# Both feed-forwards with other operands on TensorE, two norm boundaries that walk tokens 128-255 ahead, and a context scaled apart

## The chip, the cores and the metric

The kernel runs on one core of a Trainium2 chip. The metric is the device time of one execution in microseconds; lower is better. A core has a matrix engine (TensorE, PE in the profile), a vector engine (DVE), a scalar engine (ACT), GpSimd (POOL) and SyncE (SP, which here only issues transfers), an on-chip memory of 128 partitions and 8 accumulation banks of 128 x 512 f32 (PSUM, the tensor `ps`). Each engine works through its own instructions in order; semaphores are all that ties them together.

## What is computed

Two transformer blocks on 256 tokens of width 2048, in f32. The first has causal attention with 8 heads beside a gated 31-tap convolution, and a SwiGLU feed-forward; the second has neighbourhood attention with 16 heads on the tokens and 256 context tokens, and a feed-forward with a 3-tap convolution along the tokens:

```python
h = rms_norm(x, mix_pre_g) * (1 + sc1) + sh1
x = x + g1 * rms_norm(hybrid_mixer(h, ...), mix_post_g)
h = rms_norm(x, ffn_pre_g) * (1 + sc2) + sh2
x = x + g2 * rms_norm((silu(h @ w_gate) * (h @ w_up)) @ w_down, ffn_post_g)
# second block
h, hc = modulate(rms_norm(x), sh1, sc1), modulate(rms_norm(ctx), csh1, csc1)
x = x + g1 * neighbourhood_attention(h, hc, ...)
hf = modulate(rms_norm(x), sh2, sc2)
gate, up = split(dwconv3(hf @ w_up, conv_w, conv_b))
x = x + g2 * ((silu(gate) * up) @ w_down)
```

The shifts, scales and gates (sh, sc, g) are products of a vector with `ada_w`, 2048 x 12288 for each block. The hidden widths are 5632 and 5504.

## The kernel before

**Tiles of weights.** All weights pass through as tiles of 128 x 1024 f32 (512 KB). SP loads a tile into one of four `raw` slots once the low part of the tile four before is made (L352 to L365). ACT rounds it into `w_hi` (`hi`, L678, the operation is L683) once TensorE is done with the tile four before; DVE makes `w_lo = raw - w_hi` (`lo`, L1172, the operation is L1175). TensorE waits for `lo_ready`, uses the tile and raises `tile_used`. Activations are split in the same way, and a product is three matmuls: hi*hi, hi*lo, lo*hi.

**Three forms of product.** `columns_tile` (L1890, matmuls L1903 to L1905) holds a 128x128 block of weights in the array and moves the 256 tokens of `h` past it; the result has channels on the partitions. `chunk_tile` (L1858, matmuls L1873 to L1875) holds 128 tokens and moves 512 columns of weights; the result has tokens on the partitions. `row_product` (L2148, L2157 to L2159) is the same for the products `w_out` and `w_down`, one tile per 128 rows of the weight and half of the output columns. Before, both feed-forwards' gate and up products use `columns_tile`: 22 chunks of 512 columns each, 8 tiles a chunk. A loop trip of 16 tiles (`gate_up_1`, L2218) does one up and the next gate chunk.

**What is woven in.** Beside the tiles run the products of `ada_w` ("units", L1177 to L1188): SP loads 512 KB into one of two `ada` slots, DVE multiplies by the condition and adds into `acc0`, `acc1` or, for the context, `tmp` too (two operations). The schedule of units per tile is written out by hand in SP's and DVE's programs, 12 units a trip in the first two trips of the first feed-forward, 8 later. TensorE sums an accumulator over the partitions at the end (`sum_rows` L1933, `sum_columns` L1923). POOL builds the table of the second attention's bias: 16 small loads into `tab`, 8 writes of a broadcast to memory (L630), 8 skewed reads (L637), two masks (L642, L645) and a write (L647). It starts when the first boundary's x is ready.

**A boundary.** Between a `w_out` or `w_down` product and the next stage the kernel needs statistics of y (two norms), the update of x, statistics of x, and h. `last_rows` (L2162) finishes the last four tiles for tokens 128-255 first (`later_done`), then for tokens 0-127. ACT (`boundary`, L900) takes sums of squares (L882, L889, L896) and roots, DVE (L1504) updates x (L1495 to L1502) and makes a diagonal matrix of 1/rms for each half (`make_diag`, L1234); both do tokens 128-255 and then 0-127, and only then splits and h. TensorE turns x by products with the diagonals into columns (`scaled_rows`, L1941, matmul L1950), ACT scales and shifts them (`modulated`, L711, L722), DVE splits them (L1247, L1249), and `first_chunk` (L1954) starts. An f32 matmul leaves two records in the profile, a transpose one. For the second block, `first_chunk` also turns the context by diagonals behind its last tiles, and then `sum_rows` makes a gate.

**The second feed-forward's evacuation.** ACT makes the middle tap (L1124) and DVE the two outer ones (L1775, L1781) from PSUM; then `silu`, the product, and at the end `down_phase` stages its first rows (L864, L1432).

## Time and profile before

| | us |
|---|---|
| median of 3 runs | 2795.03 |
| fastest and slowest run | 2790.72, 2800.84 |
| the profiled execution | 2799.87 |
| its span, first to last instruction | 2798.2 |

| engine | busy | share |
|---|---|---|
| TensorE | 2669.5 | 95% |
| DVE | 1827.2 | 65% |
| ACT | 1275.3 | 46% |
| POOL | 143.6 | 5% |

The transfers moved 623 MB, 223 GB/s on average. Busy time of TensorE is a union of overlapping durations: a matmul's duration holds the way through the array, so its pace is read from the starts. The granted clock of TensorE, averaged over the span, was 0.976 of 2.4 GHz. The stages, in us from the start of the span: mixer to 403, its output product to 524, first feed-forward (gate and up) to 1108, down product to 1370, second block's attention to 1916, its output product to 2035, second feed-forward to 2550, down product to the end.

### The profile page before, as it was taken

The page shows a single profiled execution, that of the slowest core. Times are in us where ns is not written, and L with a number is a line of the kernel's source. Part 1 is how long each engine was busy: PE and PEld are TensorE (multiplying, and loading weights), DVE is VectorE, ACT ScalarE, POOL GpSimd, SP SyncE. Part 2 cuts the span into 40 slices and gives each one's busy share as a digit, 9 for nine tenths or more (in the row PEclk, how much of TensorE's full clock was granted, in tenths as well). Part 3 has the DMA queues.
Part 4 walks back from the last instruction along what each step waited for, and adds up shares of the span by engine and source line. Part 5 has one row for each costly group of instructions (what it writes and reads, how often), then busy time and mean ns, then how long its engine had stood idle before and what let it go on. Part 6 is the DMA issues. An engine that isn't in the chain of part 4 may idle for free.

```text
span 2798.2 us, 45510 instructions
## 1 busy us (share of the span) xinstructions
PE 2669.5 (95%) x16790; PEld 2343.3 (84%) x16790; DVE 1827.2 (65%) x2258; ACT 1275.3 (46%) x1850; POOL 143.6 (5%) x226
## 2 busy tenths in 40 slices
PE   7989898988999999999999999999999999999999
PEld 4677777888899999877777878787889999998887
DVE  2339778657788786768765555555568765656565
ACT  2349645532334243454643343434455545555553
POOL 3101011102000000000000010100000000000000
PEclk9999999999999999999999999999999999999999
DMA  9978587599788587678554454554448866655554
GB/s 342 387 271 296 187 285 248 177 291 275 257 274 274 201 282 253 223 257 299 181 172 159 161 163 153 179 176 138 160 167 287 276 193 181 183 170 177 192 192 165
DMA packets 238963, 623.03 MB, mean 223 GB/s; under 512 B 20005, under 2 KB 24256, under 8 KB 238009
## 3 DMA queue, kind: packets, MB, share of 16 engines
q1 hardware_dynamic: 210738, 519.18, 56.0%
q0 software_dynamic: 27040, 95.96, 10.4%
q10 hardware_dynamic: 1072, 6.35, 0.6%
q8 instruction: 74, 1.21, 0.2%
q14 instruction: 39, 0.32, 0.0%
HBM read 613.80 MB, written 7.60 MB: 222 GB/s over the span
## 4 chain that ended last, share of the span: by engine, by line
PE 82%; DMA 7%; DVE 5%; ACT 3%; issue 2%; SPq 0%; ACTq 0%; DVEq 0%; POOL 0%; POOLq 0%
PE ps L1903 12%; PE ps L1904 12%; PE ps L1905 12%; PE ps L2157 7%; PE ps L2158 7%; PE ps L2159 7%; PE ps L1873 6%; PE ps L1875 6%; PE ps L1874 6%; DMA ada<-in_ada_w 2%; PE ps L1986 2%; DMA raw<-in_w_up 1%; PE ps L1929 1%; ACT w_hi L683 1%; PE ps L2091 1%
## 5 line engine op out<-in xcount | busy, mean ns | idle before, releaser
L1175 DVE TENSOR_TENSOR w_lo<-raw,w_hi 128x1024 fp32r<-128x1024 f32 x766 | 938.7, 1229 | 716.9 <-ACT w_hi L683 715.7
L683 ACT ACTIVATE w_hi<-raw 128x1024 fp32r<-128x1024 f32 x766 | 811.0, 1060 | 1167.9 <-PE ps L1905 496.1
L1903 PE MATMUL ps<-h_hi,w_hi 128*128 128x256 f32 x3296 | 950.3, 288 | 36.2 <-DVE w_lo L1175 29.3
L1904 PE MATMUL ps<-h_lo,w_hi 128*128 128x256 f32 x3296 | 940.5, 285 | 0.0
L1905 PE MATMUL ps<-h_hi,w_lo 128*128 128x256 f32 x3296 | 940.0, 285 | 0.0
L1903 PEld LDWEIGHTS ps<-h_hi,w_hi 128*128 128x128 f32 x3296 | 640.5, 194 | 76.7 <-DVE w_lo L1175 36.8
L1904 PEld LDWEIGHTS ps<-h_lo,w_hi 128*128 128x128 f32 x3296 | 640.7, 194 | 0.6 <-issue 0.5
L1905 PEld LDWEIGHTS ps<-h_hi,w_lo 128*128 128x128 f32 x3296 | 640.6, 194 | 0.0
L1182 DVE SCALAR_TENSOR_TENSOR acc<-ada,cact,acc 128x1024 f32<-128x1024 f32 x224 | 291.8, 1303 | 12.6 <-DMA ada<-in_ada_w 11.0
L2157 PE MATMUL ps<-w_hi,f_hi 128*128 128x512 f32 x696 | 274.1, 394 | 14.5 <-DVE f_lo L1432 14.5
L2158 PE MATMUL ps<-w_lo,f_hi 128*128 128x512 f32 x696 | 273.0, 392 | 0.0
L2159 PE MATMUL ps<-w_hi,f_lo 128*128 128x512 f32 x696 | 272.5, 392 | 0.0
L1873 PE MATMUL ps<-w_hi,h_hi 128*128 128x512 f32 x448 | 186.7, 417 | 1.4 <-ACT ff L834 1.4
L1875 PE MATMUL ps<-w_hi,h_lo 128*128 128x512 f32 x448 | 175.8, 392 | 0.0
L1874 PE MATMUL ps<-w_lo,h_hi 128*128 128x512 f32 x448 | 175.4, 392 | 0.0
L2157 PEld LDWEIGHTS ps<-w_hi,f_hi 128*128 128x128 f32 x696 | 131.9, 189 | 44.4 <-issue 10.2
L2159 PEld LDWEIGHTS ps<-w_hi,f_lo 128*128 128x128 f32 x696 | 132.0, 190 | 27.6
L2158 PEld LDWEIGHTS ps<-w_lo,f_hi 128*128 128x128 f32 x696 | 132.1, 190 | 27.3
L1873 PEld LDWEIGHTS ps<-w_hi,h_hi 128*128 128x128 f32 x448 | 84.8, 189 | 28.4 <-issue 10.8
L1874 PEld LDWEIGHTS ps<-w_lo,h_hi 128*128 128x128 f32 x448 | 84.8, 189 | 20.6 <-issue 4.5
L1875 PEld LDWEIGHTS ps<-w_hi,h_lo 128*128 128x128 f32 x448 | 84.6, 189 | 18.4
L1873 PE MATMUL ps<-w_hi,hc_hi 128*128 128x512 f32 x256 | 99.9, 390 | 0.0
(230 smaller groups left out, 2684.9 us busy)
## 6 DMA issues: line engine op xcount, KB each, us to landing
ada<-in_w_ada SPq DMA_DIRECT2D x192, 512.0 KB, 4.3
raw<-in_ffn_w_up SPq DMA_DIRECT2D x160, 512.0 KB, 3.7
slot<-in_ada_w POOLq DMA_DIRECT2D x64, 1024.0 KB, 9.8
raw<-in_na_w_qkv SPq DMA_DIRECT2D x96, 512.0 KB, 4.7
raw<-in_w_gate SPq DMA_DIRECT2D x88, 512.0 KB, 4.8
raw<-in_w_up SPq DMA_DIRECT2D x88, 512.0 KB, 4.8
raw<-in_w_down SPq DMA_DIRECT2D x88, 512.0 KB, 5.1
raw<-in_ffn_w_down SPq DMA_DIRECT2D x86, 512.0 KB, 4.1
```

Source lines behind the costliest of these rows:

```text
L683: act.activation(w_hi[:, s, :], raw[:, s, :], ACT.Copy).then_inc(hi_ready, 1)
L1175: dve.tensor_tensor(w_lo[:, s, :], raw[:, s, :], w_hi[:, s, :].bitcast(F32), ALU.subtract).then_inc(lo_ready, 1)
L1182: ins_ = dve.scalar_tensor_tensor(out=a, in0=ada[:, half, :], scalar=cact[:, bass.ds(k + vec * KD, 1)], in1=a, op0=ALU.mult, op1=ALU.add)
L1873: pe.matmul(o, hi_[:, k, a], wh, start=(k == 0), stop=False)
L1874: pe.matmul(o, hi_[:, k, a], wl, start=False, stop=False)
L1875: mm = pe.matmul(o, lo_[:, k, a], wh, start=False, stop=(k == KD - 1))
L1903: pe.matmul(o, w_hi[:, s, a], h_hi[:, k, :], start=(k == 0 and g % 2 == 0), stop=False)
L1904: pe.matmul(o, w_hi[:, s, a], h_lo[:, k, :], start=False, stop=False)
L1905: mm = pe.matmul(o, w_lo[:, s, a], h_hi[:, k, :], start=False, stop=(k == KD - 1 and (g % 2 == 1 or g == width // P - 1)))
L2157: pe.matmul(o, fh[:, a], wh, start=first, stop=False)
L2158: pe.matmul(o, fh[:, a], wl, start=False, stop=False)
L2159: mm = pe.matmul(o, fl[:, a], wh, start=False, stop=last)
```

## The change

It has these parts.

- The first feed-forward's gate and up products take the form `chunk_tile` (tokens held, weights moved). The result has tokens on the partitions, so `u = silu(gate) * up` goes to `u_tok`, eight transposes per chunk bring it into columns in the middle of the next gate chunk, and ACT copies them to `ff`.
- The second feed-forward takes `wide_tile`: `h_hi` and `h_lo` lie in one tensor `h_both`, one matmul moves both past `w_hi` (512 columns, two halves of a bank), and one moves `h_hi` past `w_lo`. ACT copies the low half out (`z_low`), DVE adds both (`z_sum`), and the taps read that sum.
- The two boundaries with a norm become `turn`: tokens 128-255 go through statistics, update, diagonal and the first columns of h ahead of tokens 0-127, and TensorE does the first four tiles for tokens 128-255 alone and then for 0-127.
- The context is scaled by 1/rms on ACT in the down product's stage and then only transposed (`ctx_rows`), between the last four tiles of the turn; the gate's sums (`b_g1_sums`) go between the two halves of the turn, into other banks.
- POOL's table is loaded and written beside the mixer; the skewed reads wait for one tile count each, 8 tiles apart, from the 10th tile of the first feed-forward on.
- Down products: their first three rows are staged during the last up chunk; the mid-product statistics are taken for one half of the tokens at a time, the context's later still.
- Beside the two output products' attentions, one tile moves behind the first scores; the layer norm is handed over in four parts, with two units less ahead of it. Units of `ada_w` move one tile forward in the loops' steps.

```diff
+            def wide_tile(T, j0, j, part, use, width=C):
...
+                for kk in range(2):
+                    k = 2 * j + kk
+                    for g in range(width // P):
+                        a = slice(kk * width + g * P, kk * width + (g + 1) * P)
+                        pe.matmul(ps[:, 4 * part + g, :].rearrange("p (a n) -> p a n", a=2), w_hi[:, s, a],
+                                  h_both[:, :, k, :], start=(k == 0), stop=False)
+                        mm = pe.matmul(ps[:, 4 * part + g, 0:SEQ], w_lo[:, s, a], h_hi[:, k, :], start=False,
+                                       stop=(k == KD - 1))
...
+            def turn(T, target, m_, xn, n0, between=lambda: None, beside=lambda j: None):
...
+                more(0)
+                more(1)
+                for j in range(3):
+                    tile(j, (1,))
+                more(2)
+                tile(3, (1,))
+                more(3)
+                between()
+                for j in range(RING):
+                    tile(j, (0,))
+                    more(4 + j)
+                for j in range(RING, CT):
+                    tile(j, range(NT))
+                    beside(j - RING)
...
-            first_chunk(T_FF1, lambda *a: columns_tile(*a, 0, USE0["gate1"]), M["x2"], 2, 8)
+            turn(T_FF1, (*lat, 0, USE0["gate1"]), M["x2"], 2, 8)
+
+            def columns_of_u(i, bank):
+
+                pe.wait_ge(pair_free[1], i + (USE1["up1"] + 2))
+                for g in range(GH):
+                    for t in range(NT):
+                        mm = pe.transpose(ps[:, bank + g // 2, (g % 2 * NT + t) * P:(g % 2 * NT + t + 1) * P],
+                                          u_tok[:, t, g * P:(g + 1) * P], ident[:, :])
+                mm.then_inc(ut_done, 1)
...
-                    columns_chunk(T, 0, 1, i + USE1["up1"])
-                    columns_chunk(T, CT, 0, i + (USE0["gate1"] + 1))
...
+                    chunk(T, 0, [(*lat, 1, i + USE1["up1"])])
+                    chunk(T, CT, [(*lat, 0, i + (USE0["gate1"] + 1))], middle=middle)
...
+            turn(T_QKV2, (*lat, 2, USE2["qkv2"]), M["lat"], 4, 16, b_g1_sums, ctx_rows)
```

The same turn on ACT, and on DVE in the same order of halves:

```diff
+            def turn(n, phase, Tend, n0, m_, idx, beside=lambda n: None):
...
+                y_stat(n, 1, phase)
+                hi(Tend, 0)
+                x_first(phase, 1)
+                x_stat(n + 1, phase, 1)
+                act.wait_ge(tile_used, Tend + RING)
+                y_stat(n + 2, 0, phase)
+                hi(Tend, 1)
+                rows(0)
+                x_first(phase, 0)
+                rows(1)
+                hi(Tend, 2)
+                x_stat(n + 3, phase, 0)
+                hi(Tend, 3)
+                rows(2)
+                for j in range(5):
+                    rows(3 + j)
+                    hi(Tend, 4 + j)
```

The second feed-forward's evacuation, the mid-product statistics, the context and the table:

```diff
+            def z_low(pair, T, groups):
+
+                chunk_wait(T, (pair + 1) * CT)
+                act.activation(z_of[pair][:, 0:groups, :], ps[:, 4 * pair:4 * pair + groups, SEQ:2 * SEQ], ACT.Copy)\
+                    .then_inc(zlo_ready, 1)
...
+            def z_sum(pair, i, groups=GH):
+
+                dve.wait_ge(zlo_ready, 2 * i + (pair + 1))
+                z = z_of[pair][:, 0:groups, :]
+                dve.tensor_tensor(z, ps[:, 4 * pair:4 * pair + groups, 0:SEQ], z, ALU.add).then_inc(pair_free[pair], 1)
...
-                    if m == K + RING:
-                        half_stats(norm, phase)
-                        late()
+                    if m in (K + RING, K + RING + 2):
+                        half_stats(norm, phase, (int(m == K + RING),))
+                    late(m - K - RING)
...
+            def ctx_stats(o):
+                if o == 4:
+                    row_squares(2, ctx_n[1][:, :], 6, (ctx_landed, 16 * NT))
+                if o == 6:
+                    row_squares(3, ctx_n[0][:, :], 7)
+                if o in (9, 11):
+                    t = int(o == 9)
+                    act.wait_ge(ctx_std, 2 - t)
+                    act.activation(ctx_n[t][:, :], ctx_n[t][:, :], ACT.Copy, scale=stat[:, 43 - t:44 - t]).then_inc(ctx_scaled, 1)
...
             for g in range(4, GROUPS):
                 group(g)
+                if g in range(40, 48):
+                    table_heads(2 * (g - 40))
+                if g == 57:
+                    pool.wait_ge(table_landed, 16 * H2)
+                    for n in range(TABLE_PARTS):
+                        table_part(n)
...
+            pool.wait_ge(table_landed, 16 * (H2 + TABLE_PARTS))
             for n in range(TABLE_PARTS):
+                pool.wait_ge(tile_used, T_FF1 + RING + 10 + 8 * n)
...
-            out_first(T_OUT1, F_OUT1, ((0, USE0["k1"] + 2), (2, USE2["q1"] + 2)), range(2))
+            out_first(T_OUT1, F_OUT1, ((0, USE0["k1"] + 2), (2, USE2["q1"] + 2)), range(1))
```

## Rows read from the trace of the kernel before

**Rows 1.** The page: TensorE's share, then the splits of the weights (busy, mean ns).
```profile
PE 2669.5 (95%) x16790; PEld 2343.3 (84%) x16790; DVE 1827.2 (65%) x2258; ACT 1275.3 (46%) x1850; POOL 143.6 (5%) x226
...
L1175 DVE TENSOR_TENSOR w_lo<-raw,w_hi 128x1024 fp32r<-128x1024 f32 x766 | 938.7, 1229 | 716.9 <-ACT w_hi L683 715.7
L683 ACT ACTIVATE w_hi<-raw 128x1024 fp32r<-128x1024 f32 x766 | 811.0, 1060 | 1167.9 <-PE ps L1905 496.1
```

**Rows 2.** Timeline of TensorE, first feed-forward: start us, duration us, instruction.
```profile
1000.07 0.28 PE L1903 MATMUL ps<-h_hi,w_hi 128*128 128x256 f32 x1
...
1002.95 0.28 PE L1903 MATMUL ps<-h_hi,w_hi 128*128 128x256 f32 x1
```

**Rows 3.** The same, first down product.
```profile
1180.29 0.40 PE L2157 MATMUL ps<-w_hi,f_hi 128*128 128x512 f32 x1
...
1183.02 0.39 PE L2157 MATMUL ps<-w_hi,f_hi 128*128 128x512 f32 x1
```

**Rows 4.** Windows: us, PE, PEld, DVE, ACT, POOL busy, clock, DMA share, GB/s.
```profile
564.00:736.00 172.00, 149.87 (x1156) 146.87 (x1154) 112.41 (x88) 55.32 (x56) 23.54 (x16) 0.94 0.90 285
755.00:930.00 175.00, 175.00 (x1447) 175.00 (x1446) 150.22 (x132) 68.68 (x68) 0.00 (x0) 0.99 0.85 274
2090.00:2257.00 167.00, 167.00 (x1394) 167.00 (x1394) 136.83 (x162) 86.16 (x100) 0.00 (x0) 1.00 0.82 280
```

**Rows 5.** Transposes in the second attention, and the window around them (columns as above).
```profile
1490.49 1.15 PE L1919 MATMUL ps<-ident,nat_a 128*128 128x128 f32 x8 [0.25 <-ACT k_t L1073]
...
1491.71 0.39 PE L1874 MATMUL ps<-w_lo,h_hi 128*128 128x512 f32 x1
...
1489.00:1493.00 4.00, 3.75 (x25) 3.10 (x24) 0.00 (x0) 2.90 (x5) 0.00 (x0) 1.00 0.65 241
```

**Rows 6.** DMA issues, 560 to 700 and 755 to 930: median us to landing.
```profile
raw<-in_w_up SPq DMA_DIRECT2D x21, 512.0 KB, 8.0
...
raw<-in_w_up SPq DMA_DIRECT2D x27, 512.0 KB, 4.7
```

**Rows 7.** Timeline of TensorE, first trips; in brackets the idle time before.
```profile
579.47 0.58 PE L1903 MATMUL ps<-h_hi,w_hi 128*128 128x256 f32 x1 [6.47 <-DVE w_lo L1175]
...
679.56 0.39 PE L1903 MATMUL ps<-h_hi,w_hi 128*128 128x256 f32 x1 [3.49 <-DVE w_lo L1175]
...
701.74 0.58 PE L1903 MATMUL ps<-h_hi,w_hi 128*128 128x256 f32 x1 [4.29 <-DVE w_lo L1175]
```

**Rows 8.** Timelines of POOL and DVE at the masks.
```profile
672.02 6.41 POOL L642 TENSOR_SCALAR_AFFINE_SELECT skew_s<-skew_s 64x5376 f32<-64x5376 f32 x1 [7.82 <-DMA skew_s<-rpb_table]
...
679.43 6.50 DVE L1182 SCALAR_TENSOR_TENSOR acc<-ada,cact,acc 128x1024 f32<-128x1024 f32 x1
```

**Rows 9.** Timeline of ACT, first boundary: squares of y, tokens 128-255.
```profile
518.98 1.03 ACT L882 ACTIVATE junk_h<-ps 128x1024 f32<-128x1024 f32 x1 [9.57 <-PE ps L2159]
```

**Rows 10.** Timeline of TensorE at the two boundaries.
```profile
530.42 0.58 PE L1950 MATMUL ps<-diag,x 128*128 128x128 f32 x1 [6.03 <-DVE diag L1237]
...
1409.38 1.95 PE L1950 MATMUL ps<-diag,ctx_n 128*128 128x128 f32 x16
...
1419.14 0.70 PE L1938 MATMUL ps<-acc,ones 128*128 128x512 f32 x1 [3.29 <-DVE hc_lo L1249]
```

**Rows 11.** Timeline of TensorE: attentions beside output products, and the down products.
```profile
427.46 0.48 PE L2112 MATMUL ps<-ident,prob 128*128 128x128 f32 x1 [5.28 <-DVE prob L1378]
...
1111.95 0.47 PE L2157 MATMUL ps<-w_hi,f_hi 128*128 128x512 f32 x1 [3.36 <-DVE f_lo L1432]
...
1259.65 0.49 PE L2157 MATMUL ps<-w_hi,f_hi 128*128 128x512 f32 x1 [3.71 <-DVE f_lo L1432]
...
1931.52 0.33 PE L2112 MATMUL ps<-ident,prob 128*128 128x128 f32 x1 [2.12 <-DVE prob L1378]
...
2556.21 0.77 PE L2157 MATMUL ps<-w_hi,f_hi 128*128 128x512 f32 x1 [6.14 <-DVE f_lo L1432]
...
2561.00 0.39 PE L2159 MATMUL ps<-w_hi,f_lo 128*128 128x512 f32 x1
```

578 lines of the change are left out of this document (348 added, 230 removed), and 2 rows, old and new, of the table act_step.

## The prediction

> **What bounds the kernel now.** I read the page first: TensorE is busy for 95% of the span, while the splits of the weights, which DVE (L1175) and ACT (L683) make tile by tile, are 766 operations of 1.23 and 1.06 us [rows 1]. Then the timeline of TensorE, since its durations overlap and only the distance from start to start is its pace. A matmul with 256 moving columns starts every 0.120 us (24 of them, one weight tile, from 1000.07 to 1002.95) [rows 2]; one with 512 columns every 0.2275 us (12 of them, again one tile, from 1180.29 to 1183.02) [rows 3]. So a tile costs 2.88 us where the weights stand still and 2.73 us where the tokens do. Then the stages: from 755 to 930 and from 2090 to 2257 TensorE never idles, and DVE is busy for 150.2 of 175 and 136.8 of 167 us; from 564 to 736, the first three trips of the first feed-forward loop, 48 tiles at 2.88 us are 138.2 us, and the stage takes 172: 33.8 us are lost there [rows 4]. Last, from the list of waits and the timeline, where TensorE waits at the turns from one stage to the next; their rows stand with the parts below. The kernel is bound by TensorE's pace in four fifths of the span, by waits in the rest; gains in pace and gains at the turns add up, except where transfers set the time.
>
> **First feed-forward, tokens as weights.** 22 chunks of 8 tiles go from 2.88 to 2.73 us a tile: 176 x 0.15 = 26.4 us less. Added are 8 transposes in each of 11 trips, to bring u from rows to columns. Eight of them start at 1490.49 and the second matmul behind them at 1491.71 [rows 5]: 1.22 us less the 0.2275 of the first are 1.0 us, 11.0 in all. Net 15.4 us. ACT copies them out (one operation of the size of L683, 1.06 us), beside matmuls. DVE has per trip of the later stage 8 double units and 16 splits, 86% of 46.1 us now [rows 4]; of 44.7 us that is 89%, still below TensorE.
>
> These transposes are where a rule speaks against the change. Around the set of 1490 the granted clock is 1.00, which is 2.4 GHz [rows 5]. The Trainium skill (TensorE: Matmul & The Clock Gate, "Part 4: PE-mode transpose") says that transposes do not count as busy time for the clock; by it the clock could fall behind each set. The sum goes by the row, the rule is a rival below.
>
> **Second feed-forward, both halves of the tokens' split in one matmul.** For each 128x128 block three matmuls of 256 columns (0.360 us) become one of 512 and one of 256 columns. The trace of before has no 512-column matmul whose moving operand lies in two pieces. Its ends are 0.2275 us (one instruction, as in [rows 3]) and 0.240 us (two of [rows 2]); I take 0.2275, because it is one instruction and the columns follow each other at the same rate. 0.3475 us a block: 160 full tiles save 8 x 0.0125 = 0.10 us each, 16 narrow ones 0.075: 17.2 us; with the other end nothing. New beside it: a copy out of PSUM on ACT and an addition on DVE per chunk, which must be over before the taps. Both lie in order ahead of the split of the fourth tile of the next chunk. By the sizes in [rows 1] they delay it by 1.06 + 1.23 = 2.3 us, about 3.5 with the split itself, while TensorE has three tiles, 8.3 us, in hand. DVE goes from 82% to some 88% there [rows 4]. Hidden, but I charge 2 us for both feed-forwards' first chunks (ends 0 and 1 us for each of 21 chunks).
>
> **Table of the attention's bias.** Its 8 writes leave the stage at 564 for the mixer at about 290 us; the 8 reads are spread, one per 8 tiles. While they run, a weight transfer lands after 8.0 us; without them after 4.7 us [rows 6]. Of the 33.8 us lost in the first trips, 10.7 us are the three waits from 679.56 to 701.74 (3.49, 2.93, 4.29) [rows 7]: they come from the two masks on POOL, 6.4 us each, which stretch a DVE operation from 1.3 to 6.50 us [rows 8]. The masks stay, 66 tiles into the stage instead of about 41, where each unit costs DVE two operations. That stall moves and I let it grow by 2 us (ends 0 and 6). About 22 us of loss remain: the wait of 6.47 us for tile 11 [rows 7], the waits on transfers and the slow clock behind them. With 12 units and 16 tiles a trip moves 14.7 MB, at 44.7 us 328 GB/s, against 285 GB/s at 90% of the DMA engines now [rows 4], so the first two trips stay near the limit of the transfers. I take 9 of these 22 us as gained (ends 0 and 22). The writes cost the mixer 1 us (ends 0 and 8: one landing of [rows 6]).
>
> The Trainium skill (SBUF — State Buffer, on the shared port pair) says that POOL and a DVE operation with two SBUF inputs exclude each other for a whole instruction. The trace agrees with it here [rows 8], and by it the full 12.7 us of both masks stand against DVE wherever they are put.
>
> **The turns.** Before the first one ACT gets the finished half of tokens 128-255 at 518.98 [rows 9], TensorE finishes the other half at 524.2 and then waits 6.03 us for the diagonal [rows 10], because statistics and update of tokens 0-127 stand in ACT's and DVE's queues ahead of it. Now the chain of tokens 128-255 runs alone: square and root (1.03 us [rows 9], and half a microsecond for sum and root), three DVE passes of about 1.2 us (the product with the gate starts ahead of the root), square of both halves 1.5 us each: diagonal at about 526.5, 4 us sooner. What is late next is the chain of h: four scalings on ACT (1.5 us) behind the statistics of tokens 0-127 and the split on DVE, so the first product starts at about 532.2, then products of the one half cover the rest: tile 2 at 535.7, tile 4 at 549.6, chunk done at 560.5 instead of 564.1. That is 3.6 us less, 1.2 of them already counted: 2.4. The second turn has the same chain. Its context rows were diagonal products: 16 records last 1.95 us with the pipelined end of 0.28 [rows 10], so 1.7 to the next start and 7.0 for all 64; as transposes they are 32 of 0.11 us, 3.6. They lie between tiles 4 to 7, no longer behind each tile, and the sums of the gate (3.29 us of wait ahead of them, [rows 10]) go between the two halves. By the same walk the turn ends 49 us behind the first finished half instead of 58.5: 9.5 us. The two new scalings of the context on ACT, 1.9 us each, lie beside the down product, whose tiles leave ACT idle for over 1 us of 2.73. Together 11.9 (ends 3.4, the context's products alone, and 20).
>
> **Attentions beside the output products.** One tile moves behind the first scores. Before the first, two units less on DVE and a layer norm handed over in quarters let the first probabilities be ready 3.3 us sooner; the wait of 5.28 us shrinks by that. The second wait, 2.12 us, and the slow clock behind it (0.9) go [rows 11]. 6.3 us (ends 0 and 9).
>
> **Starts and middle of the down products.** Three rows are staged ahead, so the waits of 3.36 us and of 6.14 us go, the latter with 2.2 us of slow clock behind it [rows 11]; late next is the fifth tile of the second one, whose row stands behind the last taps, 2 us: 3.4 and 6.5. In the middle, statistics of both halves and of the context came in one lump, 3.71 us of wait and 3.1 of echoes and slow clock [rows 11]; they are now spread over eleven tiles: 5.5 of 6.8. Together 15.4 (ends 8 and 17).
>
> **The sum.** 15.4 + 17.2 + 9 + 11.9 + 6.3 + 15.4 = 75.2, less 2 + 2 + 1 = 5: 70.2 us. The profiled execution took 2799.9 us (span 2798.2); 2799.9 - 70.2 = 2729.7. It is 4.8 us over the median of the runs, 2795.0, so I forecast 2725.
>
> **The rivals.**
> - *The transfers keep the first trips.* For: 90% of the DMA engines busy now [rows 4]. Against: landings of 4.7 us without the table [rows 6]. Then the 9 us and the faster trips there (4.2) are not gained, and the stall of the masks grows by 4: 2742. One in ten.
> - *The transposes let the clock fall.* Behind the wait at 2556.21 eleven starts take 4.79 us, to 2561.00, 0.435 each instead of 0.2275 [rows 11]: 2.2 us. Behind each of 11 sets that is 24 us: 2749. Against: [rows 5]. The Trainium skill's rule above would do this. 5 in 100.
> - *The two-piece matmul takes 0.240 us.* The change is then not what it says in the second feed-forward: 2742. 5 in 100.
> - *Walking one half ahead gives nothing*, since ACT's scalings set the pace of the turn anyway: the 8.5 us beyond the context's products stay, 2733. 8 in 100.
> - *More is gained*: the first trips lose nothing but the masks' stall, and the turns gain 16: 2795.0 - 70.2 - 13 - 4 = 2708, or less. 12 in 100.
> - *The handover in the second feed-forward becomes the bound, and the kernel is slower.* The copy, the addition, the fourth split and the taps stand one behind another on two queues. It decides from where the fourth tile is split 8.3 us behind the chunk's end. At 12 us each of 21 chunks loses 3.7, 78 us: 2803. Against: I count 3.5 us, and DVE has 12% left. 3 in 100.
>
> **How the numbers follow.** The forecast holds 57 in 100. The range leaves out the slower end and the far side of the gains: 2698 to 2757. About 0.3% (8 us) is what a measurement of this kernel can tell from no change. Faster by more 0.95, within 0.02, slower 0.03.
>
> **What would show it.** A tile every 2.73 us in the first feed-forward, less the transposes; blocks at 0.3475 us in the second and no waits behind its chunks; TensorE's wait for the first diagonal near 2.3 us; one stretched DVE pair about 20 tiles later; no wait ahead of the down products. Wrong would make it: 0.43 us between starts behind the transposes, landings still near 8 us until 700, or waits for w_lo at each chunk of the second feed-forward.

## The result, and the profile after

| | before | after |
|---|---|---|
| median, us | 2793.18 | 2728.85 |
| fastest and slowest run | 2790.72, 2800.84 | 2717.03, 2731.99 |
| the profiled execution | 2799.87 | 2728.89 |

The ratio is 0.9757, with a 95% interval of 0.9722 to 0.9792. Between the two profiled executions 71.0 us are gained; the prediction's sum was 70.2. That agreement is partly luck, as the rest of this text shows: one term was far too small, and several others too large, by the stages by as much together.

The page of the kernel after, to be read against [rows 1]: fewer matmuls, since a tile of the first feed-forward takes 12 where it took 24, and a tile of the second 16 (its wide form needs two where three stood); and about as much work on DVE.

```profile
PE 2623.6 (96%) x13358; PEld 2151.3 (79%) x13358; DVE 1843.9 (68%) x2259; ACT 1306.8 (48%) x1869; POOL 145.0 (5%) x226
...
L1263 DVE TENSOR_TENSOR w_lo<-raw,w_hi 128x1024 fp32r<-128x1024 f32 x766 | 931.7, 1223 | 613.5 <-ACT w_hi L704 611.4
L704 ACT ACTIVATE w_hi<-raw 128x1024 fp32r<-128x1024 f32 x766 | 809.5, 1058 | 1053.5 <-PE ps L2027 350.3
```

The next view is the one to begin with after a change of many parts: each stage from its own first product on TensorE to that of the next, so that the shift of all stages ahead drops out. The columns "others" give the same stage in the experiments that leave it alone; they show how far a stage moves by itself. "TensorE's end" is the start of its last matmul. Times in us.

| from, to | before | after | gain | others of after |
|---|---|---|---|---|
| start to first output product | 403.5 | 404.1 | -0.6 | 401.4 to 405.7 |
| output product 1, start of turn 1 | 134.0 | 129.1 | 4.9 | 128.4 to 132.8 |
| rest of turn 1, first three trips, to the f32 sum | 199.4 | 167.9 | 31.5 | 166.3 to 168.9 |
| trips 3 to 6 | 196.3 | 196.8 | -0.5 | 196.8 to 197.3 |
| rest of FF1 | 178.8 | 168.5 | 10.3 | 168.1 to 171.3 |
| down product 1, start of turn 2 | 271.1 | 261.6 | 9.5 | 260.0 to 263.2 |
| rest of turn 2, qkv, attention 2 | 533.5 | 531.6 | 1.9 | 531.6 to 534.3 |
| output product 2, boundary | 128.3 | 124.4 | 3.9 | 121.0 to 125.0 |
| FF2, to the first row of down product 2 | 511.4 | 500.6 | 10.9 | 492.6 to 500.9 |
| down product 2, to TensorE's end | 236.0 | 236.6 | -0.6 | 235.6 to 237.9 |

Windows of the kernel after (us; busy of PE, PEld, DVE, ACT, POOL; clock; DMA share; GB/s), to be read against [rows 4]: the first trips need 137 us where they needed 172 and move 324 GB/s; and in FF2, 160 us hold 907 matmuls in one place and 220 us hold 1271 in another, which is a block every .353 and every .346 us, with TensorE busy all of the time in both.

```profile
564.00:701.00 137.00, 133.39 (x597) 109.26 (x596) 101.75 (x87) 55.89 (x56) 4.76 (x6) 1.00 0.93 324
755.00:890.00 135.00, 128.50 (x568) 105.88 (x567) 120.31 (x103) 52.61 (x54) 4.10 (x2) 0.97 0.88 288
2060.00:2220.00 160.00, 160.00 (x907) 138.76 (x906) 130.69 (x150) 94.50 (x108) 0.00 (x0) 1.00 0.80 262
2240.00:2460.00 220.00, 220.00 (x1271) 192.30 (x1270) 147.19 (x181) 132.57 (x152) 0.00 (x0) 1.00 0.61 183
```

The waits of TensorE after that the text speaks of, from its timeline (the idle time in brackets). In order: the first attention, the scale's sum, the two of turn 1, one behind the f32 sum, one beside the masks, one in the first down product, one at the context's transposes in turn 2, two at the head of FF2, and the first row of down product 2.

```profile
424.44 0.69 PE L2310 MATMUL ps<-ident,prob 128*128 128x128 f32 x2 [4.92 <-DVE prob L1472]
...
507.83 4.76 PE L2101 MATMUL ps<-ones,acc_s 128*128 128x1 f32 x32 [2.31 <-DVE acc_s L1283]
...
527.81 2.05 PE L2120 MATMUL ps<-diag,x 128*128 128x128 f32 x16 [2.05 <-DVE diag L1325]
...
533.21 0.50 PE L2025 MATMUL ps<-w_hi,h_both 128*128 128x512 f32 x1 [3.35 <-DVE h_both L1332]
...
716.99 0.50 PE L2025 MATMUL ps<-w_hi,h_both 128*128 128x512 f32 x1 [3.83 <-DVE w_lo L1263]
...
760.89 0.79 PE L2025 MATMUL ps<-w_hi,h_both 128*128 128x512 f32 x1 [5.66 <-DVE w_lo L1263]
...
1079.79 0.49 PE L2355 MATMUL ps<-w_hi,f_hi 128*128 128x512 f32 x1 [1.40 <-DVE f_lo L1526]
...
1360.86 0.63 PE L2504 MATMUL ps<-ident,ctx_n 128*128 128x128 f32 x4 [1.96 <-ACT h_f L751]
...
2019.43 0.50 PE L2073 MATMUL ps<-h_both,w_hi 128*128 128x512 f32 x1 [1.02 <-DVE w_lo L1263]
2024.21 0.50 PE L2073 MATMUL ps<-h_both,w_hi 128*128 128x512 f32 x1 [1.74 <-DVE w_lo L1263]
...
2484.56 0.76 PE L2355 MATMUL ps<-w_hi,f_hi 128*128 128x512 f32 x1 [4.30 <-issue]
```

The three waits of [rows 7] are gone from the first trips (the largest left there is 1.39 us; what the masks cost has moved to 760.89), and so are those of 2.99, 3.71 and 2.12 us of the kernel before ([rows 11] has the last two).

### The profile page after: what moved, and what is told of

Same layout as the page of the kernel before. It is cut to its first block, busy times and chain, and to the rows that moved or that the text cites. A ratio compares the mean times of both kernels' runs of the same rounds, so it can differ in the third digit from the quotient of the medians.

```text
span 2727.1 us, 38578 instructions
## 1 busy us (share of the span) xinstructions
PE 2623.6 (96%) x13358; PEld 2151.3 (79%) x13358; DVE 1843.9 (68%) x2259; ACT 1306.8 (48%) x1869; POOL 145.0 (5%) x226
## 4 chain that ended last, share of the span: by engine, by line
PE 81%; DMA 7%; DVE 6%; ACT 3%; issue 2%; SPq 0%; ACTq 0%; DVEq 0%; POOL 0%; POOLq 0%
PE ps L2073 11%; PE ps L2025 10%; PE ps L2027 10%; PE ps L2026 10%; PE ps L2355 7%; PE ps L2356 7%; PE ps L2357 7%; PE ps L2075 5%; PE ps L2057 2%; PE ps L2182 2%; PE ps L2058 2%; PE ps L2059 2%; DVE w_lo L1263 2%; PE ps L2101 1%; PE ps L2287 1%
## 5 line engine op out<-in xcount | busy, mean ns | idle before, releaser
L2025 PE MATMUL ps<-w_hi,h_both 128*128 128x512 f32 x1152 | 467.8, 406 | 22.5 <-DVE w_lo L1263 15.4
L2073 PE MATMUL ps<-h_both,w_hi 128*128 128x512 f32 x1376 | 483.8, 397 | 4.1 <-DVE w_lo L1263 4.1
L2027 PE MATMUL ps<-w_hi,h_both 128*128 128x512 f32 x1152 | 453.0, 393 | 0.0
L2026 PE MATMUL ps<-w_lo,h_both 128*128 128x512 f32 x1152 | 452.9, 393 | 0.0
L2075 PE MATMUL ps<-h_both,w_lo 128*128 128x256 f32 x1376 | 384.3, 279 | 0.0
L2073 PEld LDWEIGHTS ps<-h_both,w_hi 128*128 128x128 f32 x1376 | 258.9, 188 | 67.2 <-DVE w_lo L1263 5.0
L2025 PEld LDWEIGHTS ps<-w_hi,h_both 128*128 128x128 f32 x1152 | 219.0, 190 | 81.9 <-issue 17.6
L2075 PEld LDWEIGHTS ps<-h_both,w_lo 128*128 128x128 f32 x1376 | 259.8, 189 | 0.2 <-issue 0.2
L2026 PEld LDWEIGHTS ps<-w_lo,h_both 128*128 128x128 f32 x1152 | 219.2, 190 | 47.9 <-issue 4.8
L2027 PEld LDWEIGHTS ps<-w_hi,h_both 128*128 128x128 f32 x1152 | 218.9, 190 | 47.1
L2057 PE MATMUL ps<-h_both,w_hi 128*128 128x256 f32 x512 | 153.3, 299 | 6.0 <-DVE u_pad L1431 2.8
L2058 PE MATMUL ps<-h_both,w_hi 128*128 128x256 f32 x512 | 146.8, 287 | 0.0
L2059 PE MATMUL ps<-h_both,w_lo 128*128 128x256 f32 x512 | 146.6, 286 | 0.0
```

The costliest lines, as they stand in the source:

```text
L2025: pe.matmul(o, hi_[:, k, a], wh, start=(k == 0), stop=False)
L2026: pe.matmul(o, hi_[:, k, a], wl, start=False, stop=False)
L2027: mm = pe.matmul(o, lo_[:, k, a], wh, start=False, stop=(k == KD - 1))
L2057: pe.matmul(o, w_hi[:, s, a], h_hi[:, k, :], start=(k == 0 and g % 2 == 0), stop=False)
L2073: pe.matmul(ps[:, 4 * part + g, :].rearrange("p (a n) -> p a n", a=2), w_hi[:, s, a], h_both[:, :, k, :], start=(k == 0), stop=False)
L2075: mm = pe.matmul(ps[:, 4 * part + g, 0:SEQ], w_lo[:, s, a], h_hi[:, k, :], start=False, stop=(k == KD - 1))
```

## The experiments

"FF1" and "FF2" are the gate and up products of the two feed-forwards. Twelve kernels ran. In their traces a line stands a few lines off that of the kernel after.

### The table of the bias: put back, and moved alone

`table_back` is the kernel after with the table built where it was before:

```diff
-                if g in range(40, 48):
-                    table_heads(2 * (g - 40))
-                if g == 57:
-                    pool.wait_ge(table_landed, 16 * H2)
-                    for n in range(TABLE_PARTS):
-                        table_part(n)
...
-            pool.wait_ge(table_landed, 16 * (H2 + TABLE_PARTS))
+            for h in range(0, H2, 2):
+                table_heads(h)
+            pool.wait_ge(table_landed, 16 * H2)
             for n in range(TABLE_PARTS):
-                pool.wait_ge(tile_used, T_FF1 + RING + 10 + 8 * n)
+                table_part(n)
+                pool.wait_ge(table_landed, 16 * (H2 + n + 1))
```

> The changed kernel with one part undone: GpSimd builds the bias table where the kernel before did, while the first trips of FF1 run (its writes of the table to DRAM stand between w_up's landings), and no longer in the mixer's last sixteen groups. All the rest stays as changed. Theory A, that the table's traffic is what stretched the first three trips: the stretch from the gate's first matmul to the fp32 sum, 172.0 us before and 138.2 after, goes back to 158 to 168 us, the waits of TensorE for low halves return there, and the whole takes 20 to 28 us more than the changed kernel: about 2752 us. Rival B, that the row form of FF1 with its shorter TensorE work is what shortened these trips and the table costs what my forecast's term said, 9 us: the stretch takes 145 to 149 us and the whole about 2738 us. Rival C, the table is hidden anyway: within 3 us of the changed kernel, about 2729 us.

Measured: 2746.9 us, ratio 0.9839 [0.9807, 0.9870]. The first trips take 203.0 us in place of 167.9 (+35.1), trips 3 to 6 take 187.0 in place of 196.8 (-9.8), since the masks are no longer in them: 25 us net in the stages that the table touches. The median moves by 16 to 18 us only; between the two profiles other stages, which the edit leaves alone, differ by 6 us in sum the other way. Theory A comes nearest, and misses both of its windows: counted as it counts them (138.2 us in the kernel after) the first trips take 173 us, over its 158 to 168, and the whole takes 16 to 18 us more, under its 20 to 28. Rival B's 9 us are out by the stages; its 2738 us for the whole lies below the fastest of the four runs, 2742.0.

`before_table_moved` is the mirror: the kernel before, FF1 in its old form, with the same move (and with it `tab` and `skew_s` at other addresses, and DVE's wait for the table one trip later).

```diff
+                if g in range(40, 48):
+                    table_heads(2 * (g - 40))
+                if g == 57:
+                    pool.wait_ge(table_landed, 16 * H2)
+                    for n in range(TABLE_PARTS):
+                        table_part(n)
...
             for n in range(TABLE_PARTS):
+                pool.wait_ge(tile_used, T_FF1 + RING + 10 + 8 * n)
```

> The kernel before with this one part done alone: the table's heads are read and its parts written in the mixer's last sixteen groups, and the skewed copy lies 4 KB higher so that it overlaps no row of FF1 that is still to be written. FF1 keeps the column form. Theory A (the table's traffic bounds the first trips whatever the form of FF1): the first three trips fall from 172.0 us to about 150, the whole to about 2772 us. Rival B (the traffic matters only because both came together, the transfers and a TensorE that is faster in the row form): the column form's own TensorE time, 3.2 us more for three trips, hides most of it, and the gain is 9 us or less, about 2785 us. Rival C: no gain, 2793 us.

Measured: 2777.1 us, ratio 0.9946 [0.9925, 0.9967]. The first trips fall from 199.4 to 167.5 us, as low as in the kernel after, and trips 3 to 6 rise by 5.5. The whole gains 16 us, between theory A's 21 and rival B's 9, while the first trips fall by 32 us where theory A had 22. In both experiments, then, the stages say more than the medians (26 us net here, 25 above, against 16 to 18), and what makes up the difference stays open. In the first trips themselves theory A holds: the table's traffic and its masks are the whole of what was lost there, and the new form of FF1 adds nothing. In the windows TensorE is busy for 136 of 137 us in the first (the kernel before with the table moved), and for 138 of 166 us in the second (the kernel after with the table put back):

```profile
564.00:701.00 137.00, 136.06 (x1130) 135.54 (x1129) 99.24 (x86) 52.84 (x52) 4.76 (x6) 1.00 0.94 324
```

```profile
564.00:730.00 166.00, 138.40 (x571) 108.53 (x570) 105.48 (x83) 53.61 (x54) 22.84 (x16) 0.94 0.93 297
```

How much of this is transfers can be worked out from the queues (packets, MB, share of 16 engines' span); first `table_back`, 564 to 730, then the kernel after, 564 to 701. q1 carries the weights, q0 the table.

```profile
q1 hardware_dynamic: 17666, 41.96, 72.4%
q0 software_dynamic: 1523, 6.25, 19.0%
```

```profile
q1 hardware_dynamic: 17666, 41.96, 86.3%
q0 software_dynamic: 480, 1.38, 4.4%
```

The kernel before, 564 to 736, shows the same, and it was there to be read:

```profile
q1 hardware_dynamic: 17666, 41.96, 71.2%
q0 software_dynamic: 1457, 6.00, 16.4%
```

The weights take 0.724 x 166 = 120 us of the engines' time in the one and 0.863 x 137 = 118 in the other. The table takes 31.5 us in the one and 6.0 in the other: 25.5 us for 4.9 MB, 5.2 us a MB where the weights take 2.9. In the kernel before it is 0.164 x 172 = 28 us. The stage, with its DMA engines at 93%, grew by 35.1 us: these 25.5, and 9.6 that agree with the masks' share (trips 3 to 6 got shorter by 9.8).

### The masks: in parts, and left out

```diff
                 pool.dma_start(skew_s[:, n * TABLE_ROWS:(n + 1) * TABLE_ROWS, :], src).then_inc(table_landed, 16)
+                pool.wait_ge(table_landed, 16 * (H2 + TABLE_PARTS + n + 1))
+                v = skew_s[:, n * TABLE_ROWS:(n + 1) * TABLE_ROWS, 0:GRID - W]
+                link(pool.affine_select(out=v, in_=v, compare_op=ALU.is_ge, fill=NEG, base=WH,
+                                        pattern=[[0, TABLE_ROWS], [1, GRID - W]], channel_multiplier=-1))
```

and the second mask in the same way, in place of the two over the whole table.

> The changed kernel with the two masks of the skewed table, which GpSimd did in one piece each (8.16 and 6.28 us in the changed kernel's profile) over the whole table, cut in eight: each part is masked as soon as it has landed. Same arithmetic. Theory A, that the two long masks hold the two engines' shared work up (VectorE's low halves of 6.50 us beside each of them, and TensorE's waits of 5.66 and 0.85 us at 760.89 and 775.39 with the slow clock behind them): no VectorE low half of a trip takes over 4 us, the waits are gone, trips 3 to 6 take 188 to 190 us in place of 196.8, and the whole takes 7 to 9 us less than the changed kernel: about 2721 us. Rival B, the waits come from the weights' landings: they stay, and the whole is within 2 us of 2729. Rival C, sixteen short masks slow VectorE as much in sum: one wait of 5 us becomes several short ones, and half the gain is left, about 2725 us.

Measured: 2721.7 us, ratio 0.9754 [0.9728, 0.9779]; trips 3 to 6 take 189.5 us in place of 196.8. Leaving both masks out, so that the windows' edges stay unmasked, gives hardly more, 188.9 (the first of the two is shown):

```diff
-            link(pool.affine_select(out=v, in_=v, compare_op=ALU.is_ge, fill=NEG, base=WH,
-                                    pattern=[[0, H2 * DR], [1, GRID - W]], channel_multiplier=-1))
```

> The changed kernel without the two masks of the skewed bias table on GpSimd: the windows' edges are left unmasked, which is the part of the computation it leaves out, and it shows what masks cost at most. Theory A: the two VectorE low halves of 6.50 us and TensorE's waits of 5.66 and .85 us go; trips 3 to 6 take 186 to 188 us in place of 196.8. Rival B, the waits are the weights' landings: trips 3 to 6 take over 194 us.

Measured: 2722.3 us in its one run. The first expected window (188 to 190) was met, the second (186 to 188) missed by 0.9 us, and rival B, the landings, is out. What a long mask does stands in the timelines of the kernel after, first POOL, then DVE: a pass over 128x1024 of 1.28 us takes 6.50 and ends 1.1 us after the mask beside it does. These are the two passes of a unit of `ada_w`, and not low halves, as both expectations call them; the low halves wait behind them.

```profile
743.97 8.16 POOL L663 TENSOR_SCALAR_AFFINE_SELECT skew_s<-skew_s 64x5376 f32<-64x5376 f32 x1 [4.66 <-DMA skew_s<-rpb_table]
752.27 6.28 POOL L666 TENSOR_SCALAR_AFFINE_SELECT skew_s<-skew_s 64x5376 f32<-64x5376 f32 x1
```

```profile
743.23 1.28 DVE L1274 SCALAR_TENSOR_TENSOR tmp<-ada,cact,tmp 128x1024 f32<-128x1024 f32 x1
744.42 2.35 DVE L1263 TENSOR_TENSOR w_lo<-raw,w_hi 128x1024 fp32r<-128x1024 f32 x2
746.69 6.50 DVE L1270 SCALAR_TENSOR_TENSOR acc<-ada,cact,acc 128x1024 f32<-128x1024 f32 x1
753.12 6.50 DVE L1274 SCALAR_TENSOR_TENSOR tmp<-ada,cact,tmp 128x1024 f32<-128x1024 f32 x1
```

With an eighth of the table per mask, POOL and DVE (`masks_in_parts`, the last part) show the same meeting in small:

```profile
746.95 2.89 POOL L662 TENSOR_SCALAR_AFFINE_SELECT skew_s<-skew_s 64x672 f32<-64x672 f32 x1 [5.47 <-DMA skew_s<-rpb_table]
749.98 1.62 POOL L665 TENSOR_SCALAR_AFFINE_SELECT skew_s<-skew_s 64x672 f32<-64x672 f32 x1
```

```profile
749.07 1.85 DVE L1269 SCALAR_TENSOR_TENSOR acc<-ada,cact,acc 128x1024 f32<-128x1024 f32 x1
750.83 1.84 DVE L1273 SCALAR_TENSOR_TENSOR tmp<-ada,cact,tmp 128x1024 f32<-128x1024 f32 x1
```

The work of DVE lost in sum is not what counts. A pass that meets a mask now loses half a microsecond, which the three tiles in hand absorb; two passes of 6.50 us in a row, they can't.

### The first row of down product 2

```diff
-                first_row(n - CT, F_DOWN2)
+                first_row(n - CT - 3, F_DOWN2)
```

> The changed kernel with one number changed: the first row of the last down product is staged on VectorE three tiles earlier in its counting, so that it stands behind the low half that ScalarE's own order puts it behind, and no longer three low halves before ScalarE makes the high half it waits for. In the changed kernel's trace VectorE waits 4.15 us for ScalarE at 2474.13, the raw tile issued behind it lands at 2481.48, and TensorE waits 4.30 us at 2484.56, then works to 2489.95 at the slow clock. Theory A (this order is the cause): both waits and the slow clock go, and the last down product takes 234.5 to 235.5 us in place of 241.3, the whole 6 to 7 us less than the changed kernel: about 2722.5 us. Rival B, the wait is the raw tile's own landing (5.8 us there) and would come anyway: within 1.5 us of 2729.

Measured: 2724.0 us, ratio 0.9762 [0.9736, 0.9788]. The wait of 4.30 us is gone; FF2 with the start of the down product takes 487.9 us. The fair partner is the run of the kernel after further below, whose FF2 has the same pace of matmuls and takes 493.9: 6.1 us. By medians it is 5 to 7. (The expectation put the 6 to 7 us on the down product; they lie ahead of its first matmul and so count to FF2 in the table.) DVE's timeline in the kernel after shows what stood in the way: the row's low part waits for ScalarE, which makes its high part only after two more tiles, and the tiles' own low parts are queued behind it on DVE.

```profile
2474.13 0.43 DVE L1526 TENSOR_TENSOR f_lo<-ff,f_hi 128x256 fp32r<-128x256 f32 x1 [4.15 <-ACT f_hi L893]
2474.48 1.22 DVE L1263 TENSOR_TENSOR w_lo<-raw,w_hi 128x1024 fp32r<-128x1024 f32 x1
2475.91 0.42 DVE L1526 TENSOR_TENSOR f_lo<-ff,f_hi 128x256 fp32r<-128x256 f32 x1 [0.22 <-ACT f_hi L893]
2476.25 1.22 DVE L1263 TENSOR_TENSOR w_lo<-raw,w_hi 128x1024 fp32r<-128x1024 f32 x1
2482.90 0.43 DVE L1526 TENSOR_TENSOR f_lo<-ff,f_hi 128x256 fp32r<-128x256 f32 x1 [5.42 <-ACT f_hi L893]
```

Nothing runs on DVE for 5.4 us after 2477: the next tile's transfer was issued late, because its slot was freed late, and landed at 2481.5. A wait of TensorE marked "issue" began with an order of two operations on DVE 14 us before it.

### The wide matmul, and a second look at the kernel after

`wide_in_two` cuts the 512-column matmul in two:

```diff
-                        pe.matmul(ps[:, 4 * part + g, :].rearrange("p (a n) -> p a n", a=2), w_hi[:, s, a],
-                                  h_both[:, :, k, :], start=(k == 0), stop=False)
+                        pe.matmul(ps[:, 4 * part + g, 0:SEQ], w_hi[:, s, a], h_hi[:, k, :], start=(k == 0), stop=False)
+                        pe.matmul(ps[:, 4 * part + g, SEQ:2 * SEQ], w_hi[:, s, a], h_lo[:, k, :], start=False,
+                                  stop=False)
```

> The changed kernel with FF2's wide matmuls (w_hi against h_hi and h_lo side by side, 512 columns) cut back into two of 256 columns each against the same weights, 1344 blocks of them; all around stays. Theory A, my forecast's term (.3475 against .360 us a block of 128 weight rows by 256 columns, 1344 blocks): FF2 takes 16.8 us more than in the changed kernel, the whole about 2746 us. Theory B, that term holds only where nothing disturbs it, since the changed kernel's own rows show .353 a block up to 2229 us and .3465 after: FF2 takes 9 to 14 us more, the whole about 2740 us. Rival C, a block costs the same either way and FF2's gain came from elsewhere: within 3 us of 2729.

Measured: 2741.7 us, ratio 0.9819 [0.9796, 0.9843], and 509.5 us for FF2: 8.9 more than in the profile of the kernel after, but 15.5 to 17 more than in three experiments that leave FF2 alone, where it takes 492.6 to 494.0 (in `masks_out` it takes 500.9). So the stage speaks for theory A (16.8; with the 1376 blocks that the trace has, it is 17.2) or for the lower edge of theory B, depending on which profile stands for the kernel after; the whole, 2741.7, is nearer B's 2740 than A's 2746. Rival C is out. So the kernel after ran once more:

> The changed kernel once more, unchanged. In the profiles so far the first half of FF2 runs its wide blocks (512 columns, then 256) either at .3465 us a block (925 matmuls in 160 us) or at .353 (907 in 160 us), at granted clock 1.00 and with TensorE busy all of the time in both; which of the two goes with no edit. Theory A, that this is a property of the execution and of none of the edits: here the first half may show either, and FF2 up to the last down product takes 494 us where the pace is .3465 throughout, or 500 us where it is .353 in the first half; the median stays within 6 us of 2729. Rival B, that the changed kernel's own code sets it and the experiments' edits moved it: it shows .353 in the first half and .3465 in the second again, 500.5 us.

Measured: 2731.1 us, ratio 0.9777 [0.9758, 0.9796]. Its FF2 takes 493.9 us, with 867 and 868 matmuls in 150 us in its two halves. Theory A holds: the same kernel shows both paces, so the pace belongs to the execution. These are windows of the kernel after (first half slower, second faster), then of the repeat, then of `masks_out`, which has the slower pace in both halves:

```profile
2040.00:2190.00 150.00, 150.00 (x851) 130.09 (x850) 129.54 (x151) 86.19 (x100) 0.00 (x0) 1.00 0.83 280
2250.00:2400.00 150.00, 150.00 (x868) 131.12 (x867) 98.87 (x122) 88.86 (x101) 0.00 (x0) 1.00 0.64 190
```

```profile
2040.00:2190.00 150.00, 150.00 (x867) 132.28 (x866) 132.36 (x154) 89.25 (x102) 0.00 (x0) 1.00 0.86 288
2250.00:2400.00 150.00, 150.00 (x868) 131.12 (x867) 98.89 (x123) 89.25 (x102) 0.00 (x0) 1.00 0.64 190
```

```profile
2040.00:2190.00 150.00, 150.00 (x851) 130.13 (x851) 127.74 (x147) 87.98 (x101) 0.00 (x0) 1.00 0.82 274
2250.00:2400.00 150.00, 150.00 (x851) 129.99 (x850) 97.20 (x118) 87.44 (x101) 0.00 (x0) 1.00 0.62 185
```

By medians the wide form is worth 11 to 13 us, by the stage 9 to 17 with the pace of the partner. The price of .3475 us a block lies between the two paces, so this part of the term was all but right.

### The transposes, twice

```diff
-                for g in range(GH):
+                for g in (*range(GH), *range(GH)):
```

> The changed kernel with the eight transposes of every chunk of u in FF1 done twice over into the same places (160 more of them). Theory A: a transpose costs what my forecast's term said, its .11 us on TensorE with nothing else behind it: FF1 takes .88 us more for each of its chunks and quarter chunks of eight transposes, 11 us in sum over what the forecast counted, the row matmuls behind keep their step of .2275 us, and the whole is about 2740 us. Rival B, a longer stretch of transposes without matmuls lets the granted clock fall behind it: the matmuls behind each set start at twice their step for some us, and the whole is over 2760 us. Rival C, TensorE has slack there (it waits for the weights' low halves anyway): under 4 us more.

Measured: 2737.0 us, ratio 0.9812 [0.9791, 0.9833]: 6 to 8 us over the kernel after, and 9 to 10 summed over FF1's stages against its two profiles (6 against `rows_later` and `wide_in_two`), where 11 were expected. Sixteen transposes, and the first matmuls behind them:

```profile
600.47 1.91 PE L2421 MATMUL ps<-ident,u_tok 128*128 128x128 f32 x16
602.14 0.48 PE L2025 MATMUL ps<-w_hi,h_both 128*128 128x512 f32 x1
602.45 0.40 PE L2026 MATMUL ps<-w_lo,h_both 128*128 128x512 f32 x1
602.68 0.39 PE L2027 MATMUL ps<-w_hi,h_both 128*128 128x512 f32 x1
```

602.14 - 600.47 = 1.67 us for sixteen; in the kernel after, eight take 0.79 (599.56 to 600.35). So 0.11 each, and 0.31 us in place of 0.23 for the first matmul behind them. From then on the starts are 0.23 us apart, and the granted clock from 600 to 606 is 1.00. Theory A, and rival B is out: no fall of the clock follows. Rival C, under 4 us, is out too. The Trainium skill's rule that transposes don't count as busy for the clock (TensorE: Matmul & The Clock Gate, "Part 4: PE-mode transpose") has no effect that sets of 8 or 16, 1.7 us long, could show.

### TensorE without the walk ahead

```diff
-                for j in range(3):
-                    tile(j, (1,))
                 more(2)
-                tile(3, (1,))
                 more(3)
                 between()
                 for j in range(RING):
-                    tile(j, (0,))
+                    tile(j, range(NT))
                     more(4 + j)
```

> The changed kernel with TensorE's order alone put back at both boundaries: the first four tiles of the next stage are each worked for all 256 tokens at once, when both halves of the norm are there, and no more for tokens 128 to 255 ahead of 0 to 127. ScalarE, VectorE and GpSimd keep the changed order of halves. Theory A, that walking ahead is what shortens the turns: TensorE stands some 5 us longer at each turn and starts again at the slow clock; turn 1 takes 42 us in place of 37.3 and turn 2 50 us in place of 45.5, the whole about 2739 us. Rival B, that walking ahead by itself gives nothing and the turns are shorter since the context is scaled apart and the halves come in another order: both turns within 1.5 us, the whole about 2730 us.

Measured: 2734.6 us, ratio 0.9803 [0.9782, 0.9825], 4 to 6 us over the kernel after. By stages: output product 1 up to the end of the first trips 303.4 us, against 295.9 to 299.2 in the kernels with the walk (mean 297.3): 6.0; down product 1 to attention 2 799.0 against 793.1 to 797.4 (mean 794.8): 4.2, beside that scatter. Sum 10.2, as theory A says. From the last matmul of the product before it to the end of its first chunk, turn 1 takes 42.0 us in place of 37.6, and turn 2 51.3 in place of 45.7 to 48.2. The whole, 4 to 6 us more, lies halfway between theory A's 2739 and rival B's 2730: here too the stages say more than the medians. TensorE stands where the walk had given it work: it waits 2.05 us for the first diagonal and then 7.13 us for the second.

```profile
527.91 2.05 PE L2120 MATMUL ps<-diag,x 128*128 128x128 f32 x16 [2.05 <-DVE diag L1325]
...
537.09 3.79 PE L2120 MATMUL ps<-diag,x 128*128 128x128 f32 x16 [7.13 <-DVE diag L1325]
```

### The bias rows behind the weights

The wait of 3.83 us at 716.99 is in every kernel, 3.22 in the one before. The timeline of SP in the kernel after shows its cause: no tile is issued between 689.16 and 710.61, since two small loads stand ahead in the queue and wait for VectorE's memsets.

```profile
689.16 0.37 SPq L371 DMA_DIRECT2D raw<-in_w_up  x1
707.86 0.25 SPq L390 DMA_DIRECT2D acc<-in_b_ada  x1
710.00 0.25 SPq L390 DMA_DIRECT2D tmp<-in_b_ada  x1
710.61 0.41 SPq L371 DMA_DIRECT2D raw<-in_w_up  x1
```

```diff
+                        if n == 1 and rows is not None:
+                            rows()
...
-            bias_row(3, 1, b2, 0)
-            bias_row(4, 2, b2, 0)
-            ff1_loop(3, 7, ada2, 0, UNITS * 6)
+            ff1_loop(3, 7, ada2, 0, UNITS * 6, bias=lambda: both_rows(3, 0))
...
             def u_sh1(i, n):
+                if n == 0:
+                    wait_both(16)
```

> The changed kernel with one order changed that both kernels share. SyncE issues the row of a bias that goes into a cleared accumulator ahead of the next weight tiles; its issue waits for VectorE's memset, at 707.86 and 710.00 us, and the three w_up tiles behind it on SyncE's queue are issued only after 710.61, the last before them at 689.16. Here two weight tiles go ahead of the bias rows on SyncE, and VectorE waits for the bias only at the first operation that adds to it, one low half later, at four places: FF1's first trip, its trips 3 and 7, FF2's first. Theory A, this queueing is the cause of the wait of 3.83 us at 716.99 (3.22 in the kernel before) and of the short ones at the other places: trips 3 to 6 take 189 to 191 us in place of 196.8, the first three trips 2 us less, trips from the seventh on 2 us less, FF2 3 to 4 us less, the whole 12 to 15 us less than the changed kernel: about 2715 us. Rival B, VectorE's and ScalarE's own work between the trips (sum, rows, memsets) sets it: half of that, about 2722 us. Rival C: nothing, 2729 us.

Measured: 2713.5 us, ratio 0.9715 [0.9695, 0.9735], 15 to 18 us less than the kernel after. Trips 3 to 6 take 191.4 us (-5.4), the first trips 163.1 (-4.8). FF2 takes 495.4 where the kernel after took 500.6, but that is mostly pace: `halves_together`, without the edit and also with one slow half, takes 495.7. What the edit gives there is read from first halves at the faster pace, from FF2's first matmul to its 1377th: 247.3 us here and 247.4 in `all_four`, 249.0 to 249.6 in the five profiles without it, 2 us; the waits of 1.02 and 1.74 us at the head are gone. So theory A by the whole, with more at the first trips and less in FF2 than I expected.

### Together

`all_three` joins the masks in parts, the later row and this, which does two of the scale's units earlier:

```diff
-        SC2_LN, SC2_ATT, SC2_OUT = 5, (0, 1, 3, 4, 6, 7), range(11, KD + 14)
+        SC2_LN, SC2_ATT = 5, (0, 1, 3, 4, 6, 7)
+        SC2_OUT = tuple(sorted((*range(11, KD + 12), 14, 18)))
```

> The changed kernel with three small edits together: the masks done part by part, the first row of the last down product staged three tiles later, and two of the scale units of the first output product done two steps earlier, so that the last two don't hold up the sum before the first turn (wait of 2.31 us at 507.83). From the experiments so far: masks 7.3 us, rows 5 us, scale units 2 us (estimate from the one wait). Theory A, they add up, as they lie in different stages: 14 us less than the changed kernel, about 2715 us. Rival B, they overlap or the scale units only move the wait: under 9 us, above 2720 us.

Measured: 2711.8 us, ratio 0.9714 [0.9695, 0.9734], 17 to 19 us less than the kernel after; the wait of 2.31 us at 507.83 is gone and its stage takes 126.5 us, 1.9 below the lowest of the others. Theory A expected 14.

`all_four` has the bias rows behind the weights as well; its edit is that of `all_three` and of `bias_behind` together.

> The three edits and the bias rows behind the weight tiles, all together. Theory A, all add up: 26 to 29 us less than the changed kernel, about 2702 us, a ratio of .967 to the kernel before. Rival B, the bias rows' share overlaps with that of the masks (both hold up tiles of the same trips 3 and 4): 18 to 22 us less, about 2709 us.

Measured: 2689.5 us, ratio 0.9635 [0.9614, 0.9656], 39 to 42 us less than the kernel after. Theory A, and 12 us beyond it. The two parts measured apart give 32 to 37, so they overlap in nothing that shows: trips 3 to 6 get shorter by 13.6 us, by 7.3 with the masks alone and by 5.4 with the bias rows alone. Where the rest beyond 37 comes from is not shown; the mixer and output product 2, which none of the edits touches, are 6 us shorter in this profile than in the kernel after. The windows of this kernel show what is left of the first trips and of trips 3 to 6, namely next to nothing to wait for:

```profile
564.00:690.00 126.00, 126.00 (x570) 104.58 (x569) 98.43 (x84) 53.34 (x53) 21.15 (x17) 1.00 0.95 336
690.00:873.00 183.00, 181.82 (x809) 148.63 (x808) 163.06 (x142) 75.56 (x76) 8.84 (x7) 1.00 0.87 288
```

## Why the prediction was right, and where it wasn't

The forecast of 2725 us met 2728.85. By parts, gain in us:

| part | forecast | after | what showed it |
|---|---|---|---|
| FF1's form, less transposes | 15.4 | 16.7 (26.4 - 11 x 0.88) | pace 0.2275, sets of 0.88 |
| table (9, less 2 for masks, 1 for the mixer) | 6 | about 25 by stages, 16 to 18 by medians | `table_back`, `before_table_moved` |
| FF2's form, less handover | 15.2 | 9 (15 at the other pace) | `wide_in_two`, `after_again` |
| turns | 11.9 | 9.7 (2.6 and 7.1) | the stages, `halves_together` |
| attentions | 6.3 | 3.1 | the waits |
| down products | 15.4 | 8.6 | the waits, `rows_later` |

By the stages the last five rows miss by +19, -6, -2, -3 and -7: together +1, which is why the sum fits. With the table at its medians the second row would miss by some 11, and the parts come to 64 us in place of 72; the medians of the two kernels lie 64.3 apart, their profiles 71.0. The runs don't settle which of the two holds for the table, and either way its term was far too small.

**The table: the step that failed.** The prediction split the 33.8 us into 10.7 of masks and 22 of transfers, and took 9 of the 22, because the first trips would stay near the limit of the transfers, 328 GB/s being more than the 285 of then. But 285 GB/s at 90% was no limit; it was what the engines moved while a part of their time, 28 us, went to the table's small pieces. Without most of them they moved 324 at 93%, and 336 at 95% in `all_four`. The queues, taken for that stretch, say how much time that part took, and I hadn't looked at them. The upper end of my range for this term, 22, was the near one. In their new place the masks cost 7.9 us (trips 3 to 6 of `masks_out` against after; in `table_back`, where reads of the table are gone from there too, 9.8), less than the 10.7 of their old place; the growth of 2 us that I added is not seen.

**FF1's form.** Right: starts 0.2275 us apart, and 0.88 us a set of transposes where I took 1.0. DVE and ACT stay below TensorE; no wait stands behind a set. As a check with the table moved in both: FF1's three stages take 549.6 us in `before_table_moved` and 533.2 in the kernel after, 16.4 less (the first chunk of turn 1 is in both).

**FF2's form.** Right in mechanism. `h_both` in two pieces goes at 0.23 us, not 0.240; the block takes .3465 or .353 us where I took .3475. The loss of 2 us for the handover is not seen where I put it: no wait stands at a fourth tile. But the kernel after waits 1.29 us for DVE inside the gate's sum, at 2232.54, and 1.33 us near the end of FF2, at 2475.75, and the kernel before does neither; no run tried what causes them. The two waits at the head of FF2, 1.02 and 1.74, with slow starts behind them, come from the bias row ahead of the tiles.

**The turns.** By finer cuts of the same traces, from the last matmul of the product before to the end of the first chunk, turn 1 gained 2.6 us, where I had 2.4 and 1.2 by pace; turn 2 gained 7.1 of 9.5 (45.7 us for 52.8). That, too, was a good draw: in nine of the other ten profiles with the walk, turn 2 takes 47.8 to 48.2 us, since slow starts (0.43 us apart) stand behind its waits there and not here. The first diagonal comes with a wait of 2.05 us; I had said near 2.3. The wait of 3.35 us for h behind it was named as next and not hidden. The transposes of the context wait 1.96 us at 1360.86 for h of ACT, which I had not seen: on ACT their copies stand behind h.

**Attentions.** The wait of 5.28 us became 4.92, though 3.0 us earlier, since the one ahead of it (2.99 us) went; and two units of the scale, moved from ahead of the attention to the last tiles, made a new one of 2.31 us at the sum. So nothing was gained in output product 1 (-0.8, forecast 3.3). I had counted what the two units freed, and not who waits for them later; `all_three` gives that back. Output product 2 gained 3.9, forecast 3.0.

**Down products.** The first gained 7.4 of 8.9; its middle has no wait left, and what is missing is about a new wait of 1.40 us for the low part of its fifth row, at 1079.79. The second gained 1.2 of 6.5: the wait of 6.14 us became one of 4.30. I had named a later row as next late. It was the first one: the two engines stage it in different orders relative to their tiles.

The rivals: transfers that keep the first trips (324 GB/s there), a falling clock (`transposes_twice`), 0.240 us (0.23 in the windows) and a walk that gives nothing (`halves_together`, by its stages; its median alone would not do) are out. "More is gained" was right for the first trips and was offset elsewhere.

## What to carry to other kernels

Where a stage keeps its DMA engines at 90%, read the share of time of each queue, not the GB/s: 5 MB of small pieces cost 25 us of engine time here, 5 us a MB against 3. In an in-order queue ask of each waiting instruction what is queued behind it; the four small edits above are together worth 39 to 42 us, nearly two thirds of the whole change, and three of them do nothing but take a waiting instruction off the head of a queue or cut a long one in pieces. Compare a stage with several profiles of the same code before a few microseconds of it are put down to an edit. And when a sum fits, look whether its terms do.
